# Zero products at the start, later sums, and one visit per slot for the grid attention's scores, turned probabilities and values

## The chip, the cores and the metric

One core of one Trainium2 chip runs the whole program. The metric is the device time of one execution in microseconds. The engines are TensorE (PE in the rows; its weight loads are PEld), VectorE (DVE), ScalarE (ACT), GpSimd (POOL) and SyncE (SP), which issues most of the transfers.

## The reference, cut to what matters

Two transformer blocks over 512 tokens of width 1024, in fp32. The first has gated linear attention and sparse attention beside each other, then a gated feed-forward. The second has a convolution and an attention over a grid of 8 x 64 tokens, then a gated feed-forward again.

```python
h = rms_norm(x, norm_mix_pre);  proj = h @ w_in
mixed = sigmoid(merge_gla) * (o_gla @ w_proj_gla) + sigmoid(merge_nsa) * (o_nsa @ w_proj_nsa)
x = x + rms_norm(mixed @ w_out, norm_mix_post)
h = rms_norm(x, norm_ffn_pre)
x = x + rms_norm((silu(h @ w_ffn_gate) * (h @ w_ffn_up)) @ w_ffn_down, norm_ffn_post)
# second block
h = rms_norm(x, norm1_g);  a, gate, q, k, v = split(h @ w_in_2)
conv_out = silu(layer_norm(depthwise_conv31(a * sigmoid(gate)) + bias))      # over 512 channels
q, k = rms_norm per head (8 heads of 64)
attn_out = softmax(q k^T / 8 + bias over an 8 x 16 window of the grid) v
x = x + concat(conv_out, attn_out) @ w_out_2
x = x + (silu(rms_norm(x) @ w_gate) * (rms_norm(x) @ w_up)) @ w_down
```

## The kernel before, in words

**Layout.** Activations are kept transposed: channels on the 128 partitions, the 512 tokens along the free dimension, so a tile of 128 output channels is one PSUM bank of 128x512. Every large product is made of three: high part of the weight by high part of the activation, high by low, low by high (L1066 to L1068 in the plain phases, L1379 to L1381 in `block_product`). A tile with 8 blocks of 128 input channels is therefore 24 products. The phases run in the order in1, r, mgn, pg, pn, out1, gu1, dn1 (first block), in2, out2, gu2, dn2 (second block).

**The weights.** They come as 235 chunks of 128x1024, each 8 blocks. SP loads a chunk into one of two halves of `raw` (L386) once GpSimd has made the low part of the chunk that was there before; ScalarE copies it to `wH` (the high part, L505 and L517) when TensorE is through with the chunk two before; GpSimd makes `wL` = raw - wH (L427); TensorE waits for `w_lo` at the first block of each chunk. The order of the work of each engine is written out by hand; the engines meet at semaphores.

**The start.** SP issues chunk 0, the four pieces of x (L398, 128 tokens each, into `xs`) and then chunks 1 to 3, each behind what frees its half of `raw`. TensorE turns the four pieces with 32 transposes, eight a piece (L1138), waiting for `x_landed0` to `x_landed3`. ScalarE makes the high parts `aH` from the banks, in the order of `X_ORDER` (L604), VectorE the low parts `aL` (L1710), and the first tile of in1 waits for these block by block. The sum of squares follows in bank 4 behind three tiles.

**Sums.** `total` waits until all squares are added up in `ssum` and makes their sum over the channels with one product by ones (L1132). In gu1 it stands inside tile 4, behind block k == 3 (tiles 0 to 3 were made side by side, k by k). Its result goes to ScalarE (L567, L569) and VectorE (`norm`, `newton`), whose `nr` every eviction of gu1 needs. `idle_products` (L1120) are products by ones that keep TensorE at work during other roots.

**in2.** Twenty tiles (`IN2`), one chunk each, banks 0 and 1 in turn from tile 4 on, banks 2 to 7 for all else: scores in 2 and 3, turned probabilities in 4, values in 5, head norms and value turns in 6, convolution taps and the LayerNorm's sum in 7. The loop over t and k holds small work between the blocks: in each step s of `STEP_AT` (tiles 8 to 11, 13 to 16, 18 and 19, then slots of out2) the scores of 16 queries columns for a pair of heads (L1434, two matmuls of 64 rows), a tile later the four transposes of the probabilities (`turned`, L1451), a tile later again the products with the values (`values`, L1463). `value_turns` (L1420) transposes v, `head_sums` (L1390) sums the squares of q and k over a head, `head_spread` (L1405) spreads their roots over the partitions.

Per tile t, VectorE evicts tile t - 1 (L2022, L2029), runs taps of the convolution for channels 0 to 2 (L2047 for the first of a channel, L2051), `masked_max` of the step (L2065), `copied` of the step before (L2077), the reciprocals of `over_sums` (L2071), and at given tiles the head roots and `normed` (L2091). ScalarE makes the next chunk's high part (L517), squares (L864), copies of turned values (L899), exponentials (`probabilities`, L886), its taps of channel 3 (L905) and probabilities over sums (`over_sums`, L892); GpSimd adds ScalarE's taps (L484) behind its low part. ScalarE also copies a channel's finished convolution out of bank 7 (`conv_out`, L912), and VectorE may begin the next channel only then. TensorE's tile t needs the eviction of tile t - 2 (`bank_free`).

Lines that the change touches: L398 and L386 (SP), the loop over t of ScalarE behind L945, L1134 (TensorE's start), the `after` of gu1's tile 4 (before L1363), TensorE's loop of in2 with L1515, VectorE's first memset (L1623) and its loop over t (L2113 to L2122).

Of the kernel before, what the change touches and what calls it, by code (L numbers as in the profile page):

```python
# [22 lines left out]
P = 128  # L23
# [161 lines left out]
def two_blocks_kernel(nc, A):  # L185
    with ExitStack() as ctx:
# [193 lines left out]
        def _(sp):  # L380
# [12 lines left out]
            for p in PH.values():  # L393
                n4 = p.nt // 4
                if p.c0 == 0:
                    load(0, None, p.starts4[0])
                    for t in range(TT):
                        sp.dma_start(xs[:, t, :], A["x"][t * P:(t + 1) * P, :]).then_inc(sem(f"x_landed{t}"), 16)  # L398
                    for j in range(1, 4):
                        load(j % 2, j - 1 if j >= 2 else None, p.starts4[j])  # L400
# [94 lines left out]
        def _(act):  # L495
# [424 lines left out]
            for t in range(1, NT2):  # L920
# [24 lines left out]
                if t == 4:  # L945
                    act.wait_ge(sem("conv_in"), 2)
                    act.activation(yT[:, 3, :], up[:, 3, 0:S], ACT.Identity, scale=pv[:, w:w + 1], bias=vec("dw_bias", 3))\
                        .then_inc(sem("conv_mul"), 1)
                if 4 <= t < 4 + TAPS // 2:
                    taps(2 * t - 7, 2)  # L950
                if t in STEP_AT:
                    over_sums(STEP_AT[t])
                if t in SUMS_AT:
# [89 lines left out]
        def _(pe):  # L1043
# [85 lines left out]
            def total(used, bank):  # L1129

                pe.wait_ge(sem("sq_used"), used)
                pe.matmul(bank[:], ones, ssum[:], start=True, stop=True).then_inc(sem("sum_ready"), 1)  # L1132

            pe.wait_ge(sem("ones_landed"), 16)  # L1134
            for t in range(TT):
# [222 lines left out]
            for t in range(4, 8):  # L1358
                if t == 6:
                    pe.wait_ge(sem("bank_free"), NBANK + p.t0 + 1)  # L1360
                tile_products(p, 0, t, 1, aH, aL, alone=B[gu1_bank(t)], idle=True,
                              after=(lambda k: total(3 * KD, B[5]) if k == 3 else None) if t == 4 else None)
            with pe.Fori(2, p.nt // 4) as it:  # L1363
# [136 lines left out]
            for t in range(2, NT2):  # L1500
# [3 lines left out]
                for k in range(KD):  # L1504
                    if k == 1:
                        if t in STEP_AT:
                            scores(STEP_AT[t])
                        if t in VALUES_AT:
                            value_turns(VALUES_AT[t], 0)
                        if t - 1 in VALUES_AT:  # L1510
                            value_turns(VALUES_AT[t - 1], 1)
                    if k == 2 and t == NT2 - 1:
                        pe.wait_ge(sem("ln_add"), 3)
                        pe.wait_ge(sem("conv_out"), 3)
                        pe.matmul(B[7][:], ones, ssum[:], start=True, stop=True).then_inc(sem("sum_ready"), 1)  # L1515
                    if k == 2 and t in SPREAD_AT:
                        head_spread(SPREAD_AT[t], 0)
                    if k == 3 and t - 1 in STEP_AT:
                        turned(STEP_AT[t - 1])
                    if k == 4 and t in SUMS_AT:  # L1520
                        head_sums(SUMS_AT[t])
                    if k == 5 and t in SPREAD_AT:
                        head_spread(SPREAD_AT[t], 1)
                    if k == 6 and t - 2 in STEP_AT:
                        values(STEP_AT[t - 2])
                    mm = block_product(B[(p.t0 + t) % NBANK if t < 4 else t % 2], (p.c0 + t) % 2, k, aH[:, k, :], aL[:, k, :], k == 0, k == KD - 1)
# [86 lines left out]
        def _(dve):  # L1613
# [7 lines left out]

            dve.memset(nr[:, 0:1], 0.0).then_inc(sem("bank_free"), NBANK)  # L1623
            for name, n in (("gla_head", 1), ("conv_add", 2), ("ff1_fL", 2), ("ff2_fL", 2)):
# [474 lines left out]
            for t in range(1, NT2):  # L2099
# [14 lines left out]
                if t in SPREAD_AT:  # L2114
                    normed(SPREAD_AT[t], 0)
                taps(left // 2)
                left -= left // 2
                if t - 1 in STEP_AT:
                    copied(STEP_AT[t - 1])
                if t in STEP_AT:  # L2120
                    over_sums(STEP_AT[t])
                if t == 15:  # L2122
# [207 lines left out]
```

## Time and profile before

| | before |
|---|---|
| median of 3 runs | 1523.6 us (1523.14 to 1524.27) |
| the profiled execution | 1522.84 us, its span 1521.0 us |
| TensorE busy | 1499.6 us |
| VectorE, ScalarE, GpSimd busy | 664.1, 582.7, 653.5 us |
| mean granted TensorE clock | 0.996 |

A row of a timeline gives the start in us from the span's start, how long it lasted in us, engine, line, operation, what it writes and reads, and the count of merged instructions; brackets tell how long the engine sat idle before it and what released it. A fp32 matmul is two records.
### The profile page before, as it was taken

What the parts mean: (1) busy time and instruction counts of PE and PEld (TensorE: products, weight loads), DVE (VectorE), ACT (ScalarE), POOL (GpSimd) and SP (SyncE); (2) the same over time, 40 slices, a digit from 0 to 9 for tenths busy, and PEclk for the clock granted to TensorE, in tenths of its full rate; (3) what the DMA queues carried; (4) which work ended last, traced back from release to release, by engine and by line L of the source; (5) the groups of instructions that cost most, each with busy time, mean ns of one, the idle gap of its engine ahead of it and who ended that gap; (6) DMA issues with size and microseconds to landing.
All of it is one profiled execution on the core that took longest, in us unless ns stands there. A gap on an engine that the chain in (4) does not pass through costs nothing.

```text
span 1521.0 us, 20395 instructions
## 1 busy us (share of the span) xinstructions
PE 1499.6 (99%) x7388; PEld 1186.1 (78%) x7388; DVE 664.1 (44%) x1103; ACT 582.7 (38%) x912; POOL 653.5 (43%) x303
## 2 busy tenths in 40 slices
PE   7999999999999999999999999999999999999998
PEld 6888788666668877888888886777668888888887
DVE  5212344675552548433331105888756333332001
ACT  4122333654564335323332224566654333332221
POOL 3433321564134434444444543666234444444443
PEclk9999999999999999999999999999999999999999
DMA  5532211111113322333333332422113333333333
GB/s 169 165 95 67 85 42 55 42 42 56 43 56 97 97 83 84 97 97 97 97 97 97 111 105 89 153 70 58 54 56 97 97 97 97 97 97 97 111 97 111
DMA packets 40894, 135.05 MB, mean 89 GB/s; under 512 B 4464, under 2 KB 8816, under 8 KB 40576
## 3 DMA queue, kind: packets, MB, share of 16 engines
q1 hardware_dynamic: 39504, 130.56, 28.7%
q10 hardware_dynamic: 1328, 3.64, 0.8%
q8 instruction: 42, 0.69, 0.2%
q14 instruction: 20, 0.16, 0.0%
HBM read 132.09 MB, written 2.10 MB: 88 GB/s over the span
## 4 chain that ended last, share of the span: by engine, by line
PE 90%; DVE 7%; issue 1%; ACT 1%; DMA 0%; DVEq 0%; SPq 0%; ACTq 0%
PE bank L1066 21%; PE bank L1068 21%; PE bank L1067 21%; PE bank L1095 3%; PE bank L1097 3%; PE bank L1096 3%; PE bank L1379 2%; PE bank L1380 2%; PE bank L1381 2%; PE bank L1277 2%; PE bank L1296 1%; PE bank L1311 1%; DVE bank L2051 1%; DVE xT L1962 1%; DVE ssum L1645 1%
## 5 line engine op out<-in xcount | busy, mean ns | idle before, releaser
L427 POOL TENSOR_TENSOR wL<-raw,wH 128x1024 fp32r<-128x1024 f32 x235 | 574.9, 2446 | 818.8 <-ACT wH L517 642.7
L517 ACT ACTIVATE wH<-raw 128x1024 fp32r<-128x1024 f32 x209 | 221.3, 1059 | 615.0 <-PE bank L1068 574.9
L1066 PE MATMUL bank<-aH,wH 128*128 128x512 f32 x1016 | 399.2, 393 | 1.6 <-DVE aL L1710 1.1
L1067 PE MATMUL bank<-aL,wH 128*128 128x512 f32 x1016 | 396.4, 390 | 0.0
L1068 PE MATMUL bank<-aH,wL 128*128 128x512 f32 x1016 | 396.3, 390 | 0.0
L1066 PEld LDWEIGHTS bank<-aH,wH 128*128 128x128 f32 x1016 | 191.4, 188 | 47.1 <-issue 3.2
L1067 PEld LDWEIGHTS bank<-aL,wH 128*128 128x128 f32 x1016 | 191.5, 188 | 40.1 <-issue 0.7
L1068 PEld LDWEIGHTS bank<-aH,wL 128*128 128x128 f32 x1016 | 191.4, 188 | 39.9
L1066 PE MATMUL bank<-fH,wH 128*128 128x512 f32 x352 | 137.2, 390 | 0.0
L1068 PE MATMUL bank<-fH,wL 128*128 128x512 f32 x352 | 137.0, 389 | 0.0
L1067 PE MATMUL bank<-fL,wH 128*128 128x512 f32 x352 | 137.0, 389 | 0.0
L1983 DVE TENSOR_TENSOR tmp<-bank,nr 128x512 f32<-128x512 f32 x44 | 30.4, 692 | 177.8 <-PE bank L1068 176.8
L1988 DVE TENSOR_TENSOR fL<-tmp,fH 128x512 f32 (+1 forms) x44 | 80.6, 1832 | 39.2 <-ACT fH L804 39.2
L1095 PE MATMUL bank<-aH,wH 128*128 128x512 f32 x192 | 81.8, 426 | 1.1 <-DVE pj L1729 1.1
L1066 PEld LDWEIGHTS bank<-fH,wH 128*128 128x128 f32 x352 | 66.1, 188 | 13.9
L1068 PEld LDWEIGHTS bank<-fH,wL 128*128 128x128 f32 x352 | 66.1, 188 | 13.8
L1067 PEld LDWEIGHTS bank<-fL,wH 128*128 128x128 f32 x352 | 66.1, 188 | 13.4
L1097 PE MATMUL bank<-aH,wL 128*128 128x512 f32 x192 | 75.4, 393 | 0.0
L1096 PE MATMUL bank<-aL,wH 128*128 128x512 f32 x192 | 75.2, 391 | 0.0
L1379 PE MATMUL bank<-aH,wH 128*128 128x512 f32 x176 | 74.4, 423 | 0.3 <-DVE aL L2172 0.2
L1380 PE MATMUL bank<-aL,wH 128*128 128x512 f32 x176 | 68.9, 392 | 0.0
L1381 PE MATMUL bank<-aH,wL 128*128 128x512 f32 x176 | 68.9, 391 | 0.0
(302 smaller groups left out, 1872.4 us busy)
## 6 DMA issues: line engine op xcount, KB each, us to landing
raw<-in_w SPq DMA_DIRECT2D x235, 512.0 KB, 3.5
bmk<-in_bias SPq DMA_DIRECT2D x6, 512.0 KB, 4.8
pj<-in_x SPq DMA_DIRECT2D x4, 512.0 KB, 6.6
out_x<-z2T SPq DMA_DIRECT2D x8, 256.0 KB, 3.6
ct<-in_ct ACTq DMA_DIRECT2D x3, 384.0 KB, 3.2
w1k<-in_w1k ACTq DMA_DIRECT2D x1, 1024.0 KB, 5.3
w1v<-in_w1v ACTq DMA_DIRECT2D x1, 1024.0 KB, 5.1
pv<-in_pv ACTq DMA_DIRECT2D x1, 128.5 KB, 5.7
```

Of the source, the lines that this page charges most:

```text
L427: pool.tensor_tensor(wL[:, c_slot, :], raw[:, c_slot, :], wH[:, c_slot, :].bitcast(F32), ALU.subtract).then_inc(sem("w_lo"), 1)
L517: act.activation(wH[:, s, :], raw[:, s, :], ACT.Copy).then_inc(sem("w_hi"), 1)
L1066: pe.matmul(bank[:], hi, H[:, ka, :], start=(k == 0), stop=False)
L1067: pe.matmul(bank[:], hi, L[:, ka, :], start=False, stop=False)
L1068: mm = pe.matmul(bank[:], lo, H[:, ka, :], start=False, stop=(k == p.k - 1))
L1095: pe.matmul(bank[:], hi, aH[:, k, :], start=(k == 0), stop=False)
L1096: pe.matmul(bank[:], hi, aL[:, k, :], start=False, stop=False)
L1097: mm = pe.matmul(bank[:], lo, aH[:, k, :], start=False, stop=(k == KD - 1))
L1379: pe.matmul(bank[:], hi, H, start=start, stop=False, skip_group_check=True)
L1380: pe.matmul(bank[:], hi, L, start=False, stop=False, skip_group_check=True)
L1381: return pe.matmul(bank[:], lo, H, start=False, stop=stop, skip_group_check=True)
L1988: dve.tensor_tensor(fL[:, bass.ds(it * 2 + j, 1), :], tmp[:, j, :].unsqueeze(1), fH[:, bass.ds(it * 2 + j, 1), :].bitcast(F32), ALU.subtract)\
```

## The change

SP waits for the third piece of x before it issues chunk 1. VectorE writes zeros to the first half of `tmp`, and TensorE makes eight products of them into bank 7 ahead of the first transposes. The sum in gu1's tile 4 goes from behind k == 3 to behind k == 6. In in2, `turned` (one tile after the scores, at k == 3 before) and `values` (two tiles after, at k == 6 before; now three tiles after) join the scores at k == 1: scores, values, turned, then the value turns. The LayerNorm's sum goes from k == 2 to k == 4, the head sums of pair 0 from k == 4 to k == 6. ScalarE makes the probabilities over their sums ahead of its two taps; VectorE makes its reciprocals ahead of the copy, behind two taps in place of half of them.

```diff
@@ block.sync
                         sp.dma_start(xs[:, t, :], ...).then_inc(sem(f"x_landed{t}"), 16)
+                    sp.wait_ge(sem("x_landed2"), 16)
                     for j in range(1, 4):
                         load(j % 2, j - 1 if j >= 2 else None, p.starts4[j])
@@ block.scalar, in2
+                if t in STEP_AT:
+                    over_sums(STEP_AT[t])
                 if 4 <= t < 4 + TAPS // 2:
                     taps(2 * t - 7, 2)
-                if t in STEP_AT:
-                    over_sums(STEP_AT[t])
                 if t in SUMS_AT:
                     head_roots(SUMS_AT[t])
@@ block.tensor
+            pe.wait_ge(sem("zeros"), 1)
+            for _ in range(8):
+                pe.matmul(B[7][:], tmp[:, 0, 0:P], tmp[:, 0, :], start=True, stop=True, skip_group_check=True)
             pe.wait_ge(sem("ones_landed"), 16)
@@ gu1
-                              after=(lambda k: total(3 * KD, B[5]) if k == 3 else None) if t == 4 else None)
+                              after=(lambda k: total(3 * KD, B[5]) if k == 6 else None) if t == 4 else None)
@@ in2
                     if k == 1:
                         if t in STEP_AT:
                             scores(STEP_AT[t])
+                        if t - 3 in STEP_AT:
+                            values(STEP_AT[t - 3])
+                        if t - 1 in STEP_AT:
+                            turned(STEP_AT[t - 1])
                         if t in VALUES_AT:
                             value_turns(VALUES_AT[t], 0)
                         if t - 1 in VALUES_AT:
                             value_turns(VALUES_AT[t - 1], 1)
-                    if k == 2 and t == NT2 - 1:
+                    if k == 4 and t == NT2 - 1:
                         pe.wait_ge(sem("ln_add"), 3)
                         pe.wait_ge(sem("conv_out"), 3)
                         pe.matmul(B[7][:], ones, ssum[:], start=True, stop=True).then_inc(sem("sum_ready"), 1)
                     if k == 2 and t in SPREAD_AT:
                         head_spread(SPREAD_AT[t], 0)
-                    if k == 3 and t - 1 in STEP_AT:
-                        turned(STEP_AT[t - 1])
-                    if k == 4 and t in SUMS_AT:
+                    if k == (4 if SUMS_AT.get(t) else 6) and t in SUMS_AT:
                         head_sums(SUMS_AT[t])
                     if k == 5 and t in SPREAD_AT:
                         head_spread(SPREAD_AT[t], 1)
-                    if k == 6 and t - 2 in STEP_AT:
-                        values(STEP_AT[t - 2])
@@ block.vector
+            dve.memset(tmp[:, 0, :], 0.0).then_inc(sem("zeros"), 1)
             dve.memset(nr[:, 0:1], 0.0).then_inc(sem("bank_free"), NBANK)
@@ in2
-                taps(left // 2)
-                left -= left // 2
+                taps(min(left, 2))
+                left -= min(left, 2)
+                if t in STEP_AT:
+                    over_sums(STEP_AT[t])
                 if t - 1 in STEP_AT:
                     copied(STEP_AT[t - 1])
-                if t in STEP_AT:
-                    over_sums(STEP_AT[t])
```

## Rows read from the trace of the kernel before

**Rows 1.** The page, part 1: busy us, share of the span, instructions.
```profile
PE 1499.6 (99%) x7388; PEld 1186.1 (78%) x7388; DVE 664.1 (44%) x1103; ACT 582.7 (38%) x912; POOL 653.5 (43%) x303
```

**Rows 2.** Who waited for whom, TensorE: us in total, times, longest.
```profile
PE bank L1132 <- DVE ssum L1645: 1.3, 1, 1.3
PE bank L1515 <- ACT yT L912: 1.1, 1, 1.1
...
PE bank L1390 <- ACT sq L864: 0.6, 1, 0.6
```

**Rows 3.** Groups by line, VectorE: busy us, mean ns, idle before.
```profile
L1639 DVE MEMSET ssum<- 128x512 f32 x4 | 1.9, 485 | 0.2
```

**Rows 4.** Timeline of the first 16 us, VectorE and ScalarE.
```profile
0.82 0.06 DVE L1623 MEMSET nr<- 128x1 f32 x1 [0.82 <-PEq L2321]
...
11.94 3.00 ACT L604 ACTIVATE aH<-bank,pv 128x512 fp32r<-128x512 f32 x5 [5.88 <-PE bank L1138]
...
14.81 1.08 ACT L505 ACTIVATE wH<-raw 128x1024 fp32r<-128x1024 f32 x1
```

**Rows 5.** Timelines at 929 and 560 us, idle products; the window's PEclk follows POOL's.
```profile
929.19 1.88 PE L1120 MATMUL bank<-ct 128*128 128x512 f32 x4
...
560.59 3.58 PE L1120 MATMUL bank<-ct 128*128 128x512 f32 x4
...
560.70:563.90 3.20, 3.20 (x6) 1.22 (x4) 3.02 (x5) 0.92 (x2) 0.45 (x1) 0.50 0.48 138
```

**Rows 6.** The first transposes: line L1138 (ns min/median/max), all, the first eight.
```profile
L1138 PEld LDWEIGHTS bank<-ct,pj x32: 139/230/230, 6.6 to 12.1; 128*128 128x128 f32 x32
...
6.68 5.81 PE L1138 MATMUL bank<-ct,pj 128*128 128x128 f32 x32 [6.68 <-DMA pj<-in_x]
...
6.68 1.94 PE L1138 MATMUL bank<-ct,pj 128*128 128x128 f32 x8 [6.68 <-DMA pj<-in_x]
```

**Rows 7.** SP's loads of chunks 1 and 2; landing times of L386 to 20 us.
```profile
3.45 5.39 SPq L386 DMA_DIRECT2D raw<-in_w  x2
...
DMA to landing us min/median/max: 3.7/4.4/8.1
```

**Rows 8.** Timeline of gu1's tiles 4 and 5, the sum and GpSimd.
```profile
589.96 1.13 PE L1132 MATMUL bank<-ssum,ct 128*128 128x512 f32 x2 [1.27 <-DVE ssum L1645]
...
595.07 2.41 POOL L427 TENSOR_TENSOR wL<-raw,wH 128x1024 fp32r<-128x1024 f32 x1 [2.68 <-ACT wH L517]
```

**Rows 9.** Timeline of in2, TensorE: scores with value turns; values.
```profile
1001.08 0.39 PE L1381 MATMUL bank<-aH,wL 128*128 128x512 f32 x1
1001.39 0.70 PE L1434 MATMUL bank<-pk 64*128 64x256 f32 x4
1002.03 0.66 PE L1420 MATMUL bank<-ct,pk 128*128 128x128 f32 x4
1002.44 0.48 PE L1379 MATMUL bank<-aH,wH 128*128 128x512 f32 x1
...
1006.51 0.66 PE L1463 MATMUL bank<-pT,VS 128*64 128x128 f32 x8
1007.10 0.50 PE L1379 MATMUL bank<-aH,wH 128*128 128x512 f32 x1
```

**Rows 10.** VectorE in in2: two timeline rows; a window's busy us, DVE third.
```profile
1035.88 0.82 DVE L2047 TENSOR_SCALAR bank<-up,pv 128x512 f32<-128x512 f32 x1 [1.79 <-ACT yT L912]
...
1060.00 0.75 DVE L2091 SCALAR_TENSOR_TENSOR pk<-pk,pv,bank 128x512 f32<-128x512 f32 x1 [1.05 <-PE bank L1405]
...
1036.00:1058.30 22.30, 22.30 (x127) 16.95 (x125) 21.77 (x47) 14.10 (x32) 14.38 (x9) 1.00 0.25 72
```

**Rows 11.** Groups by line from 985 to 1074 us, ScalarE: busy us, mean ns.
```profile
L905 ACT ACTIVATE tmp<-up,pv 128x512 f32<-128x512 f32 x22 | 14.6, 710 | 0.0
...
L892 ACT ACTIVATE p<-p,rs 128x256 f32<-128x256 f32 x18 | 8.1, 500 | 3.0 <-DVE rs L2071 3.0
```

## The prediction

> **What bounds the kernel now.** I read the page first. TensorE is busy for 99% of the span [rows 1], so only two things can move the time: seconds in which TensorE has nothing to do or runs at its low clock, and what its own small products cost. The list of who waited for whom, TensorE alone, comes next [rows 2]: beside the wait for the input at the start it holds three waits that the change touches, 1.3 us for the sum ahead of the first feed-forward (L1132), 1.1 us for the LayerNorm's sum (L1515) and 0.6 us for the head sums (L1390). Then I read each place in the timeline. Measured start to start, with 0.23 us taken off for the block product in front, these three stalls are 1.43, 1.25 and 0.75 us.
>
> The profiled execution took 1522.84 us for its span of 1521.0; the median of the runs shown is 1523.6, so I make the sum against 1522.84 and add 0.76 at the end.
>
> **The zeros at the start.** The memset of `tmp` takes 0.49 us [rows 3] and stands where the small memset stood, at 0.82 [rows 4], so TensorE may begin at about 1.3. Each of the eight is a full fp32 product of 512 columns, and such a product is two records. Four records of the idle products take 1.88 us at the high level and 3.58 us where the granted clock reads 0.50, the 1.2 GHz level [rows 5]. Less the tail of the last record that is 0.43 us a record, 0.86 a product; at the low level twice that, 1.7. The level at the start has to be read from durations, since the granted clock reads as full before its first event: the weight loads of the first transposes take 230 ns in the median and 139 at best [rows 6], the first eight transposes come 0.215 us apart (1.94 less 0.42 for the last, over 7), and the whole 32 take 5.81 [rows 6]. With 0.109 us apart at the high level, that makes some twenty slow and eleven fast ones: the level rose about 4.4 us after the first of them.
>
> By the same delay the level would rise at 5.7 after zeros from 1.3. Until then 4.4/1.7 = 2.6 zero products are done, the other 5.4 take 4.7 us, and the zeros end at 10.4. The transposes could have begun at 6.68 [rows 6]. They then run fast: the 26th, for which ScalarE waits, starts at 10.4 + 25 x 0.109 = 13.1 where it started at 11.55 before, and ScalarE's first copy, at 11.94 now [rows 4], moves with it: **+1.5 us**. Nothing behind takes this up, since the copies, the low parts and the first products all hang on that copy. Bounds: 0 (the level rises at once, zeros end near 9, and before it had risen later in other runs) and +2.9 (it rises at 8.5); if it never rises, see the rivals. That the zeros also heat the clock for the first products is worth nothing: those ran at the high level already.
>
> Here the trace and a rule part. Eleven of these transposes ran fast after nothing but transposes [rows 6]. The Trainium skill, in TensorE: Matmul & The Clock Gate, Part 4 (PE-mode transpose), says that transposes do not engage the full clock; the trace disagrees. By that rule all 26 would have been slow before, and the term would be about 0.5 us smaller.
>
> **The wait on the third piece of x.** SP issues the loads of chunks 1 and 2 between 3.45 and 8.84 [rows 7]; now the first goes out when the third piece has landed, at about 9.2, and the second just behind it. With 4.4 us to landing [rows 7] chunk 1 is there by 13.6, and ScalarE takes it at 14.81 [rows 4], later still by the shift. Chunk 2 lands near 14 and is used at 20. Nothing, with 1.2 us of cover. If that cover is gone, the low part of chunk 1 is what comes late.
>
> **The sum of the first feed-forward, from k=3 to k=6.** Three products of 0.68 us go ahead of the wait, 2.0 us against a stall of 1.43, so the stall goes. What is late next: the sum comes out 0.6 us later (it starts at 590.57, not 589.96 [rows 8]), ScalarE's two root steps and the table load 0.6 us later, and so the high part of the chunk for tile 6, whose low part GpSimd made from 595.07 to 597.5 [rows 8]. That becomes about 598.0, and TensorE, 1.4 us early, wants it at 597.7. **-1.15 us**, between -1.43 and 0.
>
> **The visits in in2.** A visit costs its entry, its work and 0.1 us on the first product after it. From the starts in [rows 9], with 0.23 off for the product in front: scores 0.09 entry and 0.64, transposes behind them 0.41, values 0.59. Before there are 10 visits with scores (6 of them with value turns), 9 of turned and 8 of values, 27; after there are 12. Six of the eight values now stand behind scores and lose entry and exit, 6 x 0.19 = 1.1 us; the transposes have no entry of their own and lose a few hundredths each when they join a visit, 0.3 in all by my reckoning. **-1.4 us** as TensorE's own work. No row has values right behind scores; if each change of shape pays its entry and exit again, only the 0.3 is left, and the other end is -1.6.
>
> The two moved waits: head sums of tile 6 get 1.36 us more against 0.75, the LayerNorm's sum 1.36 against 1.25. **-2.0 us** more, if nothing else is late.
>
> **What comes late next.** VectorE. From 1036.0 to 1058.3 it is busy for 21.77 of 22.3 us [rows 10], and its taps are the same as before. So in2 can only get shorter if that stretch starts sooner. It starts behind a wait for ScalarE's copy of the convolution (L912), 1.79 us until 1035.88 [rows 10]. In step 4's slot ScalarE now does the probabilities over the sums (0.9 us) first and its two taps (1.3 us [rows 11]) behind them. Before, the taps filled the time in which it waited for the reciprocal. So the copy comes 1.2 us later behind that reciprocal. Following the chain back (normed keys behind the spread of tile 12, which itself now stands behind a visit of 1.2 us; the gated product; the masked maximum), the reciprocal is 1.1 us earlier: VectorE starts again at 1036.0, no sooner than now. From there the work is the same 15.3 us to the keys of pair 2, so TensorE, up to 2.5 us ahead, waits: about 0.5 us for normed keys in tile 13, 0.9 for the turned of step 5 (ScalarE ready at 1041.3, TensorE at 1040.4), 1.1 for the head sums of tile 16. Then the spread of tile 17 stands behind values and turned: VectorE's normed queries, now at 1060.00 after a wait of 1.05 [rows 10], come 0.6 later, the normed keys too, and the scores of step 8 wait some 1.3 us. In tile 10 GpSimd's taps, behind ScalarE's later ones, hold its low part 0.3 us too long. Together 4.1 us, of which 0.5 stood in the same places before; against them stands what is saved up to tile 19, 3.1 us (0.75, the visits, and in tiles 10 and 15 the values that move on to later tiles). So tile 19 starts about 0.5 us later than now. In it the LayerNorm's sum waits no more, 1.25 saved against 0.6 of values that moved in, and VectorE's copy of the turned probabilities, which held the centring, comes earlier. I take **-0.4 us** for in2 and out2 together, between -3.6 and +1.5.
>
> Sum: +1.5 - 1.15 - 0.4 = -0.05; 1522.8, and with 0.76 for the median **1523.5 us**. A measurement of this kernel can tell about 0.2%, 3.0 us, from no change.
>
> **Rivals.**
> 1. *The gains stay.* TensorE alone sets in2, because VectorE's order (reciprocal ahead of the copy) frees more than I reckon. For it: each of the waits above is under 1.5 us and worked out from a long chain. Against: the 98% of [rows 10]. 1523.6 + 1.5 - 1.2 - 3.4 = 1520.5, or 1519 if the start costs nothing. Chance 0.25.
> 2. *Slower: the zeros do not raise the level.* The place is the first 20 us. Then eight products take 13.7 us, the transposes start at 15.0 and run slowly again: the 26th at about 20, +8.4 us, 1530.8. It decides once the level rises later than 1.3 + 10 us. For it: no row has products of zeros. Against: twenty transposes were enough. Chance 0.08.
> 3. *The visits are later than I reckon* and in2 gets longer by 2 us: 1523.6 + 1.5 - 1.15 + 2 = 1526. Chance 0.12.
> 4. That the change does nothing to the start (zeros done before x lands) needs eight products in 5.4 us, 0.67 each; a record takes 0.43. Excluded.
>
> Mine has 0.55. Faster comes from rival 1, nearly whole, 0.24; slower from rival 2, a third of rival 3 and my own upper end, 0.18; the same is left with 0.58. The range, 1519.6 to 1526.9, takes in rival 1 and most of 3, leaves out rival 2.
>
> **What would show it.** First transposes at 10 to 11 and spaced 0.109 us from the first; ScalarE's first copy near 13.5. No stall at L1132, its place taken by some tenths of a microsecond ahead of tile 6. In2: twelve visits; a merged one of scores, values and turned near 1.8 us; waits at L1434 or L1451 on ScalarE and VectorE of 0.5 us and more, L1390 still waiting once, and VectorE again without a gap for 20 us. I am wrong if transposes start by 8 or after 14, or if tile 19 begins over 2 us earlier, counted from tile 2, than now.

## The result and the profile after

| | before | after |
|---|---|---|
| median of 21 runs each, beside one another | 1523.04 us | 1526.28 us |
| lowest and highest | 1521.40, 1524.64 | 1522.33, 1526.74 |
| the profiled execution, its span | 1522.84, 1521.0 | 1526.74, 1524.9 |
| mean granted clock of the profiled execution | 0.996 | 0.994 |

The ratio, taken over all executions, is 1.0017, 95% interval 1.0011 to 1.0023: the change makes the kernel 2.6 us slower (the medians alone lie 3.2 apart), where I forecast no change (-0.05 on the sum of the steps). It is little, but its interval leaves out one. The profiled executions lie further apart, 3.9 us, and that difference is what the traces can explain piece by piece.

TensorE still fills the span. Part 1 of the page, after, beside [rows 1]:

```profile
PE 1508.3 (99%) x7404; PEld 1190.9 (78%) x7404; DVE 667.0 (44%) x1104; ACT 583.4 (38%) x912; POOL 653.3 (43%) x303
```

The start, in the timelines of TensorE, VectorE and ScalarE (start, duration, engine, line, operation, in brackets the idle time before it and its releaser):

```profile
0.92 0.48 DVE L1628 MEMSET tmp<- 128x512 f32 x1 [0.92 <-PEq L2327]
...
1.46 9.15 PE L1138 MATMUL bank<-tmp 128*128 128x512 f32 x16 [1.46 <-DVE tmp L1628]
10.45 3.66 PE L1143 MATMUL bank<-ct,pj 128*128 128x128 f32 x32
15.17 0.47 PE L1067 MATMUL bank<-aH,wH 128*128 128x512 f32 x1 [1.07 <-DVE aL L1716]
...
13.55 3.00 ACT L605 ACTIVATE aH<-bank,pv 128x512 fp32r<-128x512 f32 x5 [7.73 <-PE bank L1143]
```

The transposes wait no longer for x, which was there at 6.68 [rows 6], but for the zeros, until 10.45. They are fast, 3.66 us for all, and ScalarE's first copy stands at 13.55, not 11.94 [rows 4].

Who waited for whom, TensorE, us in total, times, longest:

```profile
PE bank L1439 <- DVE pk L2097: 1.8, 2, 1.3
...
PE bank L1524 <- ACT yT L913: 1.1, 1, 1.1
...
PE bank L1067 <- POOL wL L428: 0.9, 1, 0.9
...
PE bank L1384 <- POOL wL L428: 0.3, 1, 0.3
```

Against [rows 2], the wait of the first feed-forward's sum and that of the head sums are gone; the LayerNorm's sum waits as long as before; new are two waits for normed keys (L1439) and two for GpSimd's low parts (L1067, L1384).

The 5544 block products, those with the high or the low part of a weight, stand in the same order in both traces, so each can be set beside its twin. The shift is how much later a product starts after than before. It is +1.62 us at the first product of in1. It is +1.69 ahead of gu1's sum and +1.82 behind gu1's tile 7, +2.28 at the first product behind the root before in2, +1.64 in in2's tile 7, behind the head sums of tile 6, +2.36 behind those of tile 19, and +3.96 four blocks on, where it stays to the end. Two of the steps up, at the root ahead of in2 and at the end of in2, coincide with a fall of the clock. Two windows of the changed kernel (length, then busy us of PE, PEld, DVE, ACT, POOL, the granted clock, DMA):

```profile
930.57:933.98 3.41, 3.41 (x7) 1.87 (x8) 2.24 (x4) 0.80 (x2) 1.00 (x1) 0.50 0.39 115
1084.17:1087.58 3.41, 3.41 (x9) 2.62 (x9) 3.31 (x9) 2.04 (x5) 0.00 (x0) 0.50 0.00 0
```

A granted clock of 0.50 is the 1.2 GHz level. The first window lies mostly in idle products, and the step there is 0.5 us; in the second the block products come 0.43 us apart in place of 0.23, and that is the 1.6 us.

### The profile page after: what moved, and what is told of

It reads as the page before. It is cut to its first block, busy times and chain, and to the rows that moved or that the text cites. A ratio compares the mean times of both kernels' runs of the same rounds, so it can differ in the third digit from the quotient of the medians.

```text
span 1524.9 us, 20428 instructions
## 1 busy us (share of the span) xinstructions
PE 1508.3 (99%) x7404; PEld 1190.9 (78%) x7404; DVE 667.0 (44%) x1104; ACT 583.4 (38%) x912; POOL 653.3 (43%) x303
## 4 chain that ended last, share of the span: by engine, by line
PE 75%; issue 14%; DVE 5%; POOL 4%; ACT 1%; POOLq 0%; DVEq 0%; ACTq 0%
PE bank L1067 18%; PE bank L1068 18%; PE bank L1069 18%; POOL wL L428 3%; PE bank L1384 2%; PE bank L1385 2%; PE bank L1386 2%; PE bank L1096 2%; PE bank L1098 2%; PE bank L1097 2%; PE bank L1439 1%; PE bank L1246 1%; DVE bank L2057 1%; PE bank L1282 1%; PE bank L1138 1%
## 5 line engine op out<-in xcount | busy, mean ns | idle before, releaser
L1067 PE MATMUL bank<-aH,wH 128*128 128x512 f32 x1016 | 399.2, 393 | 2.7 <-DVE aL L1716 1.1
L1067 PEld LDWEIGHTS bank<-aH,wH 128*128 128x128 f32 x1016 | 191.4, 188 | 49.5 <-issue 3.7
L1067 PE MATMUL bank<-fH,wH 128*128 128x512 f32 x352 | 137.2, 390 | 0.0
L1067 PEld LDWEIGHTS bank<-fH,wH 128*128 128x128 f32 x352 | 66.1, 188 | 13.9
L1384 PE MATMUL bank<-aH,wH 128*128 128x512 f32 x176 | 73.2, 416 | 0.6 <-POOL wL L428 0.3
```

What stands on the lines that cost most here:

```text
L1067: pe.matmul(bank[:], hi, H[:, ka, :], start=(k == 0), stop=False)
L1384: pe.matmul(bank[:], hi, H, start=start, stop=False, skip_group_check=True)
```

## The experiments

Each experiment was timed beside the kernel before on the same chip; its medians there were 1523.02 (e1 to e4), 1523.51 (e5 to e8), 1522.75 (e9 to e12) and 1523.30 us (e13 to e16). The ratios are against those, so kernels of different groups are compared by their ratios.

### The three parts, each alone

**e1: the start alone.**

```diff
+                    sp.wait_ge(sem("x_landed2"), 16)
+            pe.wait_ge(sem("zeros"), 1)
+            for _ in range(8):
+                pe.matmul(B[7][:], tmp[:, 0, 0:P], tmp[:, 0, :], start=True, stop=True, skip_group_check=True)
+            dve.memset(tmp[:, 0, :], 0.0).then_inc(sem("zeros"), 1)
```

> The kernel before with the start alone: SP's wait for the third piece of x, the memset of tmp and the eight zero products. Theory A (the zeros end after x has landed and push ScalarE's first copy from 11.94 to 13.55, and nothing behind takes that up): +1.6 us in the median, zeros from 1.5 to 10.4, the 32 transposes in 3.7 us. Theory B (the time comes from in2 and the start is made good later): within 0.5 us of the kernel before. Theory C (a low-level stretch of the granted clock is moved to another place, or one more comes, by the shift of everything behind): +1.6 and up to 1.7 more in executions whose mean granted clock is 0.002 lower.

Measured: 1524.79 us, ratio 1.0011 (1.0002 to 1.0020). That is +1.7 us, Theory A, though the profile has ScalarE's first copy at 14.47, 0.9 us later than in the changed kernel with the same eight products. What differs is when the level rose: the first six gaps between the zeros' records are 0.85 us or more here, the first four there. Theory C gets nothing: the mean granted clock is 0.9965, beside 0.9963 for the kernel before.

**e2: gu1's sum alone.**

```diff
-                              after=(lambda k: total(3 * KD, B[5]) if k == 3 else None) if t == 4 else None)
+                              after=(lambda k: total(3 * KD, B[5]) if k == 6 else None) if t == 4 else None)
```

> The kernel before with the sum of gu1 behind k == 6 alone. My prediction was -1.15 us. Theory A (the wait of 1.3 us only moves: 0.3 us for the low part of tile 5's chunk and 1.05 for that of tile 7, both GpSimd behind ScalarE's later copy): 0.0 within 0.3 us, with no stall at the sum's product and two stalls of together 1.3 to 1.4 us on GpSimd's low part at 592 and 603 us. Theory B (the stall is gone when the start is as before): -1.0 to -1.4 us.

Measured: 1523.16, ratio 1.0000 (0.9991 to 1.0009). The shift against the kernel before is -0.07 us ahead of the sum and +0.07 behind tile 7 of gu1: the part gains nothing at all. Theory A.

**e3: in2 alone**, all its lines of the diff shown ahead, nothing at the start or in gu1.

> The kernel before with all of the change in in2 and nothing of it elsewhere. Theory A (in2's own gains and waits cancel, as in my prediction, and the 1.7 us on top came from a low-level stretch of the granted clock at 1084 us): -0.1 us within 0.6 where no such stretch falls into in2, +1.6 where one does; mean granted clock tells them apart. Theory B (the waits of VectorE's chain make in2 longer by themselves): +1.5 us or more at the clock of the kernel before.

Measured: 1522.68, ratio 1.0003 (0.9994 to 1.0012). In its trace the shift moves by -0.65 over the head sums of tile 6 and by +0.71 from there to behind those of tile 19, together +0.06; then a stretch of low clock at 1077.6 adds 1.6. Theory A.

**e4: the change without the zeros.**

```diff
-            pe.wait_ge(sem("zeros"), 1)
-            for _ in range(8):
-                pe.matmul(B[7][:], tmp[:, 0, 0:P], tmp[:, 0, :], start=True, stop=True, skip_group_check=True)
-            dve.memset(tmp[:, 0, :], 0.0).then_inc(sem("zeros"), 1)
```

> The changed kernel without its zeros (no memset, no products), SP's wait for x kept. If SP's wait costs nothing and the zeros cost 1.6 us: 1.6 us below the changed kernel's median of 1526.3, so 1524.7. If the low-level stretches follow from the shift by 1.6 us that the zeros cause: down to 1522.9, at a mean granted clock of 0.996 and without the stretch at 1084 us.

Measured: 1523.30, ratio 1.0000 (0.9991 to 1.0009). Without the zeros the change costs nothing that can be measured (the interval is 1.4 us to either side): they carry the 2.6 us, more than the 1.6 that one pair of profiles showed. The time lies 3.0 below the changed kernel's, between the two that I had expected and nearer the lower one. There is no low stretch at 1084 in its trace, but one execution does not tell whether the zeros' shift has to do with that.

### What the start costs

The weight loads of the transposes (ns min, median, max; first and last start) tell how early the level rose. First e4, then a kernel whose start is the one of before (e8 below):

```profile
L1139 PEld LDWEIGHTS bank<-ct,pj x32: 139/142/230, 6.7 to 11.4; 128*128 128x128 f32 x32
```

```profile
L1138 PEld LDWEIGHTS bank<-ct,pj x32: 140/226/229, 6.7 to 12.8; 128*128 128x128 f32 x32
```

Same code, and the last transpose is 1.4 us apart. In the nine traces without zeros (before, e2, e3, e4, e7, e8, e11, e12, e14), 13 to 27 of the 31 gaps between transposes are slow, and ScalarE's first copy comes between 10.94 and 12.58, at 11.66 in the mean. With eight zeros (after, e1, e5, e13) it comes at 13.55, 14.47, 14.46 and 14.59, 14.27 in the mean: **+2.6 us**. The kernel before happened to show 11.94 and the changed one 13.55, the earliest of its four. With three or four zeros (e6, e9, e10, e15, e16 below) it comes at 10.77 to 11.07, at 10.89 in the mean.

**e6: four zero products in the changed kernel.**

```diff
-            for _ in range(8):
+            for _ in range(4):
```

> The changed kernel with four zero products, not eight. Theory A (only their end behind x's landing costs; the level rises about 4.3 us after the first whatever follows): zeros from 1.5 to 7.0, the transposes 0.109 us apart from 7.0 with a wait for a piece of x between, ScalarE's first copy near 10.5, the median 3 us below the changed kernel's, 1523.3. Theory B (four products do not raise the level before the transposes): transposes 0.215 us apart as before, first copy at 12 to 12.5, the median 1.3 us below, 1525.

Measured: 1521.64, ratio 0.9987 (0.9978 to 0.9995). First copy at 10.92. Timeline of TensorE:

```profile
1.46 6.52 PE L1137 MATMUL bank<-tmp 128*128 128x512 f32 x8 [1.46 <-DVE tmp L1627]
7.82 3.66 PE L1142 MATMUL bank<-ct,pj 128*128 128x128 f32 x32
```

The zeros end 0.8 us later than I expected, since seven of the eight records ran at the low level; the transposes are 0.109 us apart. Theory A. By the ratios it is 4.6 us faster than the changed kernel, where I had expected 3; the first copies give 3.4 of that (14.27 less 10.89), and the mean granted clock is higher, 0.9964 against 0.9950.

Four more kernels have every stall removed that the other parts aim at (e10, below) and differ in the start alone.

**e13: eight zeros.** `range(4)` becomes `range(8)`.

> The kernel with four zeros, gu1's two edits, head sums behind k == 6 and the LayerNorm's sum behind k == 4, but with eight zero products. Theory A (only the end of the zeros counts): ScalarE's first copy at 13.5 to 14.5 us, 3.0 us above the kernel with four (1516.7), so 1519.7, and 2.5 above the one without any. Theory B (most of the 2.6 us of the change came from waits elsewhere that this kernel does not have): less than 1.5 us above the one without any.

Measured: 1520.95, ratio 0.9984 (0.9975 to 0.9993), 1.2 us above what I had expected. Timeline of TensorE:

```profile
1.46 10.19 PE L1137 MATMUL bank<-tmp 128*128 128x512 f32 x16 [1.46 <-DVE tmp L1627]
11.49 3.66 PE L1142 MATMUL bank<-ct,pj 128*128 128x128 f32 x32
16.21 0.47 PE L1067 MATMUL bank<-aH,wH 128*128 128x512 f32 x1 [1.06 <-DVE aL L1715]
```

Against e10 the shift is +3.52 us at the first block product and +3.53 at the last of the kernel: what the start loses arrives at the end in full.

**e14: no zeros.** The wait, the loop and the memset are left out.

> The same kernel without zeros (SP's wait kept). Theory A (four zeros save what the slow transposes cost, 0.7 us in the mean of the first copies): first copy at 11 to 12.5 us, 1517.4. Theory B (zeros never pay, since the clock rises at a time of its own): within 0.3 us of the kernel with four.

Measured: 1519.09, ratio 0.9967 (0.9956 to 0.9978), first copy at 11.28. So eight zeros cost 0.0017 of the time, 2.6 us, against none (1.9 between the medians), also where none of the changed kernel's waits in in2 are left: Theory A of e13. That four are better than none is not settled by the times: this one's start (first product at 12.89) is 0.2 us later than that of e10, and the rest of the 2.3 us between the two traces are the low stretches at 112 and 560 us, which differ from one execution to the next. The first copies speak for four, by 0.8 us in the mean.

**e15: four zeros, without SP's wait.**

```diff
-                    sp.wait_ge(sem("x_landed2"), 16)
```

> The same kernel with four zeros and without SP's wait for the third piece of x. My prediction: the wait costs nothing and gives nothing, 1516.7 within 0.4. Rival (it keeps the loads of chunks 1 and 2 off the queues while x lands): x's first piece lands later than 6.5 to 6.9 us and ScalarE's first copy comes later by the same.

Measured: 1518.04, ratio 0.9962 (0.9948 to 0.9975), first copy at 10.77 against 11.07 with the wait. No use of the wait is to be seen; x's pieces came no later without it (6.4 us from issue to landing in the median, 6.7 in e10). The median is above my 1516.7 within 0.4, but the interval holds e10's ratio of 0.9954.

**e16: three zeros.** `range(4)` becomes `range(3)`.

> The same kernel with three zero products, which end at 6.7 us at the low level, as x's first piece lands. Theory A (TensorE goes from zeros to transposes without a gap and the level rises 3 to 6 us after the first product whatever it computes): first copy at 10.3 to 11.2 us, 1516.3 to 1516.7. Theory B (the transposes hold the rise back): first copy at 11.5 or later.

Measured: 1517.13, ratio 0.9957 (0.9943 to 0.9970), first copy at 10.81. Timeline of TensorE:

```profile
1.46 4.38 PE L1137 MATMUL bank<-tmp 128*128 128x512 f32 x6 [1.46 <-DVE tmp L1627]
6.62 1.06 PE L1142 MATMUL bank<-ct,pj 128*128 128x128 f32 x8 [0.77 <-DMA pj<-in_x]
7.83 3.52 PE L1142 MATMUL bank<-ct,pj 128*128 128x128 f32 x24 [0.15 <-DMA pj<-in_x]
```

The transposes run fast from the first on, and TensorE waits for each piece of x. Theory A; as good as four.

### Where the stall of gu1 went

Timelines of the changed kernel in gu1, TensorE, GpSimd and ScalarE:

```profile
592.26 1.02 PE L1133 MATMUL bank<-ssum,ct 128*128 128x512 f32 x2
...
593.59 0.40 PE L1069 MATMUL bank<-aH,wL 128*128 128x512 f32 x1
594.13 0.50 PE L1067 MATMUL bank<-aH,wH 128*128 128x512 f32 x1
...
606.23 0.50 PE L1067 MATMUL bank<-aH,wH 128*128 128x512 f32 x1 [0.89 <-POOL wL L428]
...
591.69 2.39 POOL L428 TENSOR_TENSOR wL<-raw,wH 128x1024 fp32r<-128x1024 f32 x1 [5.42 <-ACT wH L518]
...
603.80 2.38 POOL L428 TENSOR_TENSOR wL<-raw,wH 128x1024 fp32r<-128x1024 f32 x1 [4.29 <-ACT wH L518]
...
602.13 0.63 ACT L801 ACTIVATE sq<-sq 128x512 f32<-128x512 f32 x1 [1.42 <-DVEq L1987]
602.67 1.05 ACT L518 ACTIVATE wH<-raw 128x1024 fp32r<-128x1024 f32 x1
```

The sum's product starts 0.23 us behind the one in front: no stall. But tile 5 begins 0.54 us behind its forerunner, as the low part of its chunk ends at 594.08, and tile 7 waits from 605.2 to 606.2 for the low part begun at 603.80. ScalarE makes that chunk's high part behind the second gate's activation (L801), which hangs on VectorE's eviction, that on the root, and that on the sum. 0.3 and 1.06 us, measured start to start, are nearly the 1.43 that the stall had.

**e7: e2 and ScalarE's high part ahead of that activation.**

```diff
                     high_f(0, 0)
-                    silu(0, 1)
                     ahead(p, 1, 1)
+                    silu(0, 1)
                     high_f(0, 1)
```

> The kernel before with the sum of gu1 behind k == 6 and, in ScalarE's order, the high part for tile 7's chunk ahead of the second gate's activation. Theory A (the stall moved to GpSimd's low part for tile 7, late behind ScalarE's copy): that stall of 1.05 us goes, 0.3 us for tile 5 stays, the time is 1.0 us below the kernel before at the same clock, and the shift against it measured at the end of gu1 is -1.0. Theory B (the evictions, which wait for the root, set the pace): the shift at the end of gu1 stays at 0 within 0.2, with a wait for a bank in place of the wait for the low part.

Measured: 1521.47, ratio 0.9994 (0.9985 to 1.0003). Timelines of ScalarE and GpSimd:

```profile
598.03 1.05 ACT L517 ACTIVATE wH<-raw 128x1024 fp32r<-128x1024 f32 x1
...
599.16 2.41 POOL L427 TENSOR_TENSOR wL<-raw,wH 128x1024 fp32r<-128x1024 f32 x1 [2.25 <-ACT wH L517]
```

Tile 7 waits no more; tile 5's 0.3 us stands in the starts as before. Over gu1 the shift against the kernel before goes from -0.90 to -1.98, where that of e2 goes from -0.07 to +0.07: the two edits gain 1.1 us, Theory A. Two medians are too coarse to show it by themselves.

### Where in2's gains went

One joined visit of the changed kernel, and the one that waits longest, TensorE's timeline:

```profile
1034.96 0.39 PE L1386 MATMUL bank<-aH,wL 128*128 128x512 f32 x1
1035.28 0.70 PE L1439 MATMUL bank<-pk 64*128 64x256 f32 x4
1035.91 0.66 PE L1468 MATMUL bank<-pT,VS 128*64 128x128 f32 x8
1036.50 0.66 PE L1456 MATMUL bank<-ct,p 128*128 128x128 f32 x4
1036.91 0.48 PE L1384 MATMUL bank<-aH,wH 128*128 128x512 f32 x1
...
1066.83 0.39 PE L1386 MATMUL bank<-aH,wL 128*128 128x512 f32 x1
1068.50 0.70 PE L1439 MATMUL bank<-pk 64*128 64x256 f32 x4 [1.28 <-DVE pk L2097]
...
1079.79 0.39 PE L1386 MATMUL bank<-aH,wL 128*128 128x512 f32 x1
1081.32 1.10 PE L1524 MATMUL bank<-ssum,ct 128*128 128x512 f32 x2 [1.14 <-ACT yT L913]
1082.26 1.84 PE L1395 MATMUL bank<-ct,sq 128*128 128x2 f32 x16
1083.96 0.60 PE L1384 MATMUL bank<-aH,wH 128*128 128x512 f32 x1
1084.35 0.63 PE L1385 MATMUL bank<-aL,wH 128*128 128x512 f32 x1
1084.78 0.63 PE L1386 MATMUL bank<-aH,wL 128*128 128x512 f32 x1
```

The visit costs 1.72 us and 0.09 on the next product, 1.81; as three visits [rows 9] the same work cost 0.83, 0.79 and 0.45, 2.07. The values have no entry of their own behind scores. Over all visits of tiles 8 to 19, less the stalls, TensorE's own small work, all time above 0.23 us a block product, falls from 29.3 to 27.8 us.

And VectorE's restart and its normed queries, and ScalarE's last copy of the convolution, in their timelines; the last row is that copy in the kernel before:

```profile
1037.81 0.81 DVE L2053 TENSOR_SCALAR bank<-up,pv 128x512 f32<-128x512 f32 x1 [2.69 <-ACT yT L913]
...
1061.96 0.75 DVE L2097 SCALAR_TENSOR_TENSOR pk<-pk,pv,bank 128x512 f32<-128x512 f32 x1 [0.93 <-PE bank L1410]
...
1080.60 0.58 ACT L913 ACTIVATE yT<-bank 128x512 f32<-128x512 f32 x1
...
1076.40 0.59 ACT L912 ACTIVATE yT<-bank 128x512 f32<-128x512 f32 x1
```

**e8: only the head sums of pair 0, from k == 4 to k == 6.**

```diff
-                    if k == 4 and t in SUMS_AT:
+                    if k == (4 if SUMS_AT.get(t) else 6) and t in SUMS_AT:
```

> The kernel before with only the head sums of pair 0 moved from k == 4 to k == 6 of tile 6. Theory A (VectorE's chain sets in2 from tile 11 on, so what TensorE gains ahead of it is given back): the shift is -0.75 to -1.0 us behind tile 6 and back to within 0.3 of zero by tile 19, the median as before. Theory B (TensorE sets in2): -0.75 stays to the end, 1522.3.

Measured: 1522.08, ratio 0.9991 (0.9982 to 0.9999). The shift goes from -0.98 ahead of the moved sums to -1.62 behind them, and stays at -1.62 for 72 us, until a stretch of low clock at 1053. Its VectorE starts the next channel so:

```profile
1034.29 0.81 DVE L2047 TENSOR_SCALAR bank<-up,pv 128x512 f32<-128x512 f32 x1 [1.79 <-ACT yT L912]
```

That is the same wait of 1.79 as in [rows 10], 1.59 earlier: it follows TensorE. Theory B. VectorE's chain does not hold in2 to the old time. (The time of the profiled execution says less: with the stretch at 1053 its shift is 0 at the end.)

**e11: the orders of ScalarE and VectorE alone** (on e8; the lines of the diff shown ahead under the scalar and the vector block).

> The kernel before with the head sums behind k == 6 and only the orders of ScalarE (probabilities over their sums ahead of its taps) and VectorE (two taps, reciprocals, then the copy) as changed; no visit joined. Theory A (ScalarE's later taps make its copy of the convolution late, 2.7 us of wait for VectorE in place of 1.8, and so the normed keys and the LayerNorm's sum): the waits of 0.5 and 1.3 us for normed keys are there, VectorE waits 2.7 us for ScalarE's copy, the shift from tile 7 to tile 19 is +1 to +2 us. Theory B (it is the visit of 1.8 us that holds TensorE's own products back): shift within 0.3, no waits for normed keys.

Measured: 1522.24, ratio 1.0001 (0.9992 to 1.0010). VectorE waits 2.67 us for ScalarE's copy and against e8 the shift grows by 1.0 us from tile 7 to 1052, as Theory A has it. But there is no wait for normed keys, so those come from elsewhere: neither theory as it stands.

**e12: the joined visits alone** (on e8; the lines of TensorE's k == 1, orders as before).

> The kernel before with the head sums behind k == 6 and only the visits joined (scores, values of three steps back, turned of one back at k == 1); ScalarE's and VectorE's orders as before. Theory A (a joined visit is cheaper by 0.19 us where values join and by some hundredths where the turned do, 1.4 us in all): TensorE's products of tiles 8 to 19 take 1.2 to 1.4 us less, but the turned wait for ScalarE's probabilities, whose order is still taps first: shift from tile 7 to tile 19 between -1 and +1. Theory B (each change of shape pays again): no more than 0.3 us less of TensorE's own work, shift positive by the waits.

Measured: 1522.67, ratio 0.9998 (0.9989 to 1.0007). TensorE's waits:

```profile
PE bank L1434 <- DVE pk L2091: 1.8, 2, 1.3
PE bank L1451 <- ACT p L892: 1.1, 1, 1.1
PE bank L1519 <- ACT yT L912: 1.1, 1, 1.1
```

The normed keys are late because of the visits: the spread of the roots stands behind a longer visit, and VectorE's normed tiles behind the spread. Against e8 in2 is 1.2 us longer (the shift goes from +0.63 at tile 7 to +0.19 at the end, over the 1.63 of low clock that e8 has and e12 has not). The turned wait as Theory A has it; the 1.8 us for the normed keys were not in it. By themselves, then, the orders cost about 1 us and the visits 1.2, while both together, with the LayerNorm's sum behind k == 4, cost 0.7 (+1.64 to +2.36 above): with the orders the turned probabilities no longer wait.

**e5: the LayerNorm's sum behind k == 6, in the changed kernel.**

```diff
-                    if k == 4 and t == NT2 - 1:
+                    if k == 6 and t == NT2 - 1:
```

> The changed kernel with the LayerNorm's sum behind k == 6 of tile 19, not k == 4. Theory A (the sum still waited 1.3 us at k == 4 since ScalarE's copy of the convolution comes later, and the wait, the sum and the 16 products of the head sums, now next to each other, let TensorE's clock fall behind them): the wait is gone, the clock keeps its level at 1084 us, the median falls by 1.3 us and, where the level would have fallen, by 1.6 more: 1523.4 to 1525 against the changed kernel's 1526.3. Theory B (the level falls by chance of the phase, and what is late behind the sum takes up the gain): 1525.5 to 1526.5, with a new stall in out2.

Measured: 1525.74, ratio 1.0013 (1.0004 to 1.0021). Its own wait is gone; the head sums of tile 19, now ahead of it, wait 0.6 us, and behind both the shift against the changed kernel is down by 0.45. But in out2 the sums over the channels now wait for VectorE:

```profile
PE bank L1107 <- DVE ssum L1650: 1.0, 1, 1.0
```

and the level falls at 1082.6 all the same, and once more at 1092.8. The shift against the changed kernel is 2.3 us higher at the end than ahead of tile 19's sums; the wait in out2 is 1.2 of that and the second stretch 1.5. The median lies in the range of Theory B, and the new stall is its own. That the sum's place next to the head sums makes the clock fall is not borne out.

### Two kernels from the parts that pay

**e9: four zeros and SP's wait, e7's two edits, e8's head sums;** visits, orders and LayerNorm as in the kernel before.

> The kernel before with what paid by itself: four zero products and SP's wait, gu1's sum behind k == 6 with the high part for tile 7 ahead of the second gate, head sums of pair 0 behind k == 6; in2 otherwise untouched. Theory A (the three add up: -0.7 at the start against the mean of the profiles without zeros, -1.0 in gu1, -0.65 in in2): 2.3 us below the kernel before, 1521.0, interval below 1.0. Theory B (the phase of the low-level stretches takes it back): within 1 us of the kernel before.

Measured: 1518.16 (1516.15 to 1519.83), ratio 0.9966 (0.9954 to 0.9979): 5.2 us faster, more than twice my 2.3. The shift of the traces is -3.33. The mean granted clock of its six executions is 0.9985, that of the 22 of the kernel before beside them 0.9964. Its trace has one stretch of low clock before the last microseconds, the kernel before's has two. So the low stretches gave more, where Theory B feared that they would take back; why, no run here isolates. For scale: of the kernel before, the 34 executions with a mean clock of 0.998 took 1522.4 us in the mean and the 23 with 0.994 took 1524.5, so 0.0021 of clock goes with about 1.1 us.

**e10: e9 with the LayerNorm's sum behind k == 4.**

> The same kernel with the LayerNorm's sum behind k == 4 as well. Theory A (with ScalarE's and VectorE's order of before its convolution copy is not late, so the stall of 1.25 us goes): 1.2 us below the kernel beside it, 1519.8, no wait at the sum. Theory B (the sum next to the head sums lets the level fall at 1080 us, or out2 gives the gain back): same as the one beside it or 0.5 us above, with a low-level stretch or new waits behind 1083 us.

Measured: 1516.69 (1514.73 to 1517.11), ratio **0.9954 (0.9940 to 0.9968)**, the fastest: 7.0 us below the kernel before (6.1 between the medians). From 930 to 1130 us TensorE's list holds nothing but this:

```profile
PE bank L1438 <- DVE aL L2177: 0.5, 1, 0.5
PE bank L1438 <- issue: 0.3, 1, 0.3
PE bank L1383 <- DVE aL L2177: 0.2, 1, 0.2
```

The step between its trace and that of e9 at the LayerNorm's sum is -1.3 us. There the same edit does what it did not do in the changed kernel, and it stands next to the head sums with the clock at full level. Theory A.

## Why the prediction was wrong

**The zeros: +1.5 forecast, +2.6 found.** The mechanism held to the tenth of a microsecond: zeros from 1.46 (1.3 forecast) to 10.45 (10.4), the copy at 13.55 (13.5). What failed is the sum made from one execution: I read the moment at which the level rises from one trace and carried it over as fixed. It varies, over 1.6 us in the first copies without zeros. In the mean the copy comes 0.3 us earlier without zeros than in the trace that I read (11.66, 11.94) and 0.8 later with eight than I forecast (14.27, 13.5). That the forecast met the profiled execution so closely was luck: it is the earliest of four. The upper bound, +2.9, holds the mean. Rival 2 (the level never rises) fell; its 26th transpose should stand at 20.4, not 20, for its 1530.8. Of the rule that I weighed: in e3, 18 of 31 gaps are fast behind nothing but slow transposes, so transposes do raise the level. The Trainium skill, TensorE: Matmul & The Clock Gate, Part 1 (The HAM clock gate), has the other half, which I did not use: it says that the number of slow products at the start of the same kernel differs between executions. Here the trace agrees, with 13 to 27 slow gaps.

**SP's wait: nothing.** Right (e15), with 0.3 us the other way in the first copy.

**gu1's sum: -1.15 forecast, +0.1 found.** This is the step that failed outright: "That becomes about 598.0, and TensorE, 1.4 us early, wants it at 597.7". I followed ScalarE's chain to the next chunk only, tile 6's. Tile 5's low part, behind the squares and not behind the sum at all, was already 0.3 us late for an earlier TensorE, and tile 7's hangs on sum, root, eviction and activation, so that in e2 it starts 0.3 us later (602.05 against 601.76) while TensorE comes 1.1 us earlier. The low part of tile 6's chunk, the one that I followed, did not hold TensorE up. My bound of 0 for the gain was reached. Rival 1 counted on this gain and missed it.

**The visits: -1.4 forecast, -1.5 found.** Right, and so is the reason: the values have neither entry nor exit of their own.

**The moved waits: -2.0 forecast, -0.65 found.** The head sums' stall is gone (-0.64 in the pair of traces and in e8, 0.75 forecast). The LayerNorm's is not: "In it the LayerNorm's sum waits no more" failed, as ScalarE's copy of the convolution comes 4.2 us later than before (1080.60 against 1076.40), when TensorE's shift there is under 3. With the old order it is in time (e10).

**What comes late next: +3.6 forecast, +2.35 found.** Normed keys in tile 13: 0.5 forecast, 0.56 found; step 8: 1.3 and 1.35; the low part in tile 10: 0.3 and 0.44. The turned of step 5 (0.9) and the head sums of tile 16 (1.1) do not wait. I had them hang on "VectorE starts again at 1036.0, no sooner than now". Counted from in2's first product it starts 0.35 us sooner (1037.81 less 2.28, against 1035.88), and e8 shows it starting sooner when TensorE does; what frees those two beyond that, no run isolates. Rival 1, which left out these waits and expected 3.4 us from in2, fell on them. Over in2 the errors cancel: -0.4 forecast for it and out2, +0.1 found in the traces of the changed kernel and of e3, +0.3 in that of e4, where no low stretch falls on the end of in2. My -0.4 did not follow from my own terms either: -1.4, -2.0 and +3.6 make +0.2.

**Together.** +2.6, +0.1 and +0.1 make 2.8; the ratio's 1.0017 is 2.6. Of the gap to my -0.05, 1.1 us were lost at the start, 1.25 in gu1 and 0.5 in in2. Rival 3 had the total right (1526) by a mechanism that did not occur. The 1.3 us by which the profiled pair differs beyond that are the two more stretches of low clock, 0.5 and 1.6, less the start's luck. The 21 executions of the changed kernel have a mean granted clock of 0.9950, 109 of the kernel before 0.9961. By the scale given at e9 that goes with some 0.6 us of the 2.6, which is not in the sum, so the sum meets the ratio closer than it should; four first copies with eight zeros do not fix their mean to half a microsecond. Whether the change itself brings more such stretches stays open.

## What to carry to other kernels

Cover ahead of a transfer should be counted at the slowest clock that it can meet, and end about when the transfer lands. Behind three products the transposes began at 6.62 us, behind four at 6.80 to 7.82, and the first copy came at 10.8 to 11.1 in both cases; behind eight they began at 10.45 to 11.49, and what was lost there stood at the end of the kernel. A stall that is covered by earlier work only moves unless each consumer of the chain behind it has slack: follow it over several chunks, and look also at producers that never depended on it, for the engine now arrives there earlier. A term whose size hangs on the moment of a clock change needs more than one trace.

## What was not expected of the hardware

The stretches at a granted clock of 0.50 stand at other places from trace to trace of nearly the same work: at 113 and 560 us before, at 115, 562, 931 and 1084 after, at 114 alone in e10. Among block products one cost up to 1.6 us. In e9, with its three parts improved, the mean clock was 0.9985 in place of 0.9964, and the gain twice what the parts were worth by forecast; that the one brings the other was not tested by itself. A loss of 3.52 us in the first 16 us, measured at the last product 1500 us later, was 3.53.
